# Splitting w_out beside the last token block, with the GLU parts in two buffers and chunk 1 loaded behind them

## What is computed

```python
h = rmsnorm(x, norm_pre_mix);  proj = h @ w_in
u, z, xbc, dt_raw, qk, v, i_raw, f_raw, o_raw = split(proj)
y_a = s5_mixer(u, ...)      # 32 groups x 16 channels, complex state; then g * sigmoid(g @ w_glu + b_glu)
y_b = ssd_mixer(z, xbc, dt_raw, ...)                 # 12 heads x 64, 2 groups, state 128, chunks of 128
y_c = mlstm_mixer(qk, v, i_raw, f_raw, o_raw, ...)   # 6 heads, keys 64, values 128
x = x + rmsnorm(concat[y_a, y_b, y_c] @ w_out, norm_post_mix)
h = rmsnorm(x, norm_pre_ffn)
out = x + rmsnorm((silu(h @ w_gate) * (h @ w_up)) @ w_down, norm_post_ffn)
```

## Time and profile before

| | |
|---|---|
| Timed runs | 3061.14, 3063.23, 3067.11 us |
| Profiled execution | 3071.86 us, span on the core 3070.1 us |
| Busy share of the span | TensorE 94%, VectorE 62%, ScalarE 39%, GpSimd 13% |
| VectorE in tenths, slices of 77 us | 3 from 998 to 1074 us, 4 from 1074 to 1151 us |
| Weight split L1576, mean of its group | 1345 ns |
| Load of `m_bc`, median to landing | 6.9 us |
| Token stage, last tile | about 1123.5 us |
| Mixers | 1124 to about 1490 us |

### The profile page before, as it was taken

The page is one execution under the profiler, slowest core; times in us unless marked ns, Lnnn a source line. Parts: engine busy times, 40 slices in busy tenths (PEclk is TensorE's granted clock), DMA queues, the critical chain, the costliest instruction groups (busy, mean ns, idle before and its releaser), DMA issues. The chain is left out here.

```text
span 3070.1 us, 36078 instructions
## 1 busy us (share of the span) xinstructions
PE 2893.7 (94%) x13608; PEld 2329.9 (76%) x13608; DVE 1918.2 (62%) x2608; ACT 1200.5 (39%) x2000; POOL 390.4 (13%) x495
## 2 busy tenths in 40 slices
PE   7999999799999888999699859999999999999998
PEld 4788887577777666777488748888878888888887
DVE  4677877575652348888334467666676666556756
ACT  5322222354343344544234343333443333444543
POOL 0000000013440225665012100000000000000100
PEclk9999999899999988999799979999999999999999
DMA  4222433336666737776568654444543222776863
GB/s 149 66 66 87 128 128 104 117 133 204 215 202 187 237 103 248 265 278 245 203 250 307 235 195 168 158 158 158 182 174 130 103 103 105 270 247 195 297 192 110
DMA packets 295289, 545.14 MB, mean 178 GB/s; under 512 B 59308, under 2 KB 150860, under 8 KB 286284
## 3 DMA queue, kind: packets, MB, share of 16 engines
q1 hardware_dynamic: 263356, 437.69, 42.5%
q0 software_dynamic: 24704, 75.52, 6.8%
q10 hardware_dynamic: 7056, 29.63, 2.4%
HBM read 358.30 MB, written 184.44 MB: 177 GB/s over the span
## 5 line engine op out<-in xcount | busy, mean ns | idle before, releaser
L2530 PE MATMUL f_banks<-f_bop,f_w_op 128*128 128x512 f32 x3696 | 841.2, 390 | 31.5 <-DVE f_w_op L2357 29.5
L2530 PEld LDWEIGHTS f_banks<-f_bop,f_w_op 128*128 128x128 f32 x3696 | 695.4, 188 | 177.3 <-DVE f_w_op L2357 29.9
L2538 PE MATMUL f_banks<-f_d_op 128*128 128x512 f32 x1848 | 419.0, 389 | 0.0
L2538 PEld LDWEIGHTS f_banks<-f_d_op 128*128 128x128 f32 x1848 | 346.8, 188 | 72.0
L2421 DVE TENSOR_TENSOR f_d_op<-f_d_raw,f_d_op 128x1024 fp32r<-128x1024 f32 x154 | 187.5, 1225 | 149.0 <-ACT f_d_op L2274 148.3
L1708 PE MATMUL t_banks<-t_w_hi,h_hi 128*128 128x512 f32 (+1 forms) x640 | 249.4, 390 | 26.4 <-DVE t_w_lo L1576 26.4
L640 PE MATMUL c_banks<-h_hi,c_w_hi 128*128 128x512 f32 x640 | 255.7, 400 | 0.0
L640 PE MATMUL c_banks<-h_hi,c_w_lo 128*128 128x512 f32 x640 | 249.9, 391 | 0.0
L640 PE MATMUL c_banks<-h_lo,c_w_hi 128*128 128x512 f32 x640 | 249.1, 389 | 0.0
L2274 ACT ACTIVATE f_d_op<-f_d_raw 128x1024 fp32r<-128x1024 f32 x154 | 162.9, 1061 | 198.3 <-PE f_banks L2538 161.6
L1708 PE MATMUL t_banks<-t_w_lo,h_hi 128*128 128x512 f32 (+1 forms) x640 | 239.6, 374 | 0.0
(11 more groups left out here) (350 smaller groups left out, 4620.6 us busy)
## 6 DMA issues: line engine op xcount, KB each, us to landing
f_raw<-in_w_gu SPq DMA_DIRECT2D x88, 512.0 KB, 6.4
sop<-f_a SPq DMA_DIRECT2D x154, 256.0 KB, 2.0
f_d_raw<-sop SPq DMA_DIRECT2D x154, 256.0 KB, 2.8
t_raw<-in_w_tok SPq DMA_DIRECT2D x72, 512.0 KB, 4.4
f_d_raw<-top SPq DMA_DIRECT2D x88, 256.0 KB, 3.8
m_bc<-rows SPq DMA_DIRECT2D x16, 1152.0 KB, 6.9
f_d_raw<-in_w_dn SPq DMA_DIRECT2D x66, 256.0 KB, 3.0
o_y_hi<-y_hi SPq DMA_DIRECT2D x16, 1024.0 KB, 5.1
```

What stands on the lines that cost most here:

```text
L2530: last = nc.tensor.matmul(bank[:, g, :], w_op[:, t % W_RING, w, cols], bop[:, s, h, k, :], start=begins and k == 0 and j == 0, stop=k == 3 ...
L2538: last = nc.tensor.matmul(banks[:, bank, :], d_op[:, d % D_RING, s, tok], d_op[:, d % D_RING, w, :], start=k == 0 and j == 0, stop=k == FU ...
```

## The change

**GLU parts.** `y_hi` and `y_lo` have two buffers each, by the parity of the part; `y` is written into the buffer of `y_lo` and overwritten by the difference. The semaphore of the stores is split by parity, and a part waits for the store of part n - 2 instead of n - 1.

**w_out.** The six pieces are loaded, copied and split in the token stage: load g at slot 116 + 4g on SyncE, copy and split at slot 118 + 4g on ScalarE and VectorE, behind whatever else the slot holds. There is one raw buffer instead of two, so a load waits for the split before it; the other half of `gate_rows` becomes `m_va` of even chunks.

**Chunk 1.** `m_w_hi` and `m_w_lo` must now lie clear of the token stage. In their place the second buffers of `bc`, `ch`, `tk`, `zo`, `va`, and xde, xskip, h and others, overlap with it. So chunk 1 is loaded in `rest()`, and GpSimd's xde and xskip of chunk 0 and VectorE's memset of h follow the last tile.

**Waits.** `tokens_done` is now the tiles' products alone. A new `stores_done` (tiles copied and stored, GLU parts stored) is awaited by SyncE before the loads of chunk 1, by ScalarE before the first squares, by GpSimd behind the first products, and by VectorE before the first write of `y`.

```diff
@@ mixer_memory @@
-        sb("pad_a", [P, 110])
...
+        sb("pad_a", [P, 640])
+        bc1, ch1 = sb("bc1", [P, NBC, P]), sb("ch1", [P, CT - CH0, P])
...
+        w_hi, w_lo = sb("w_hi", [P, NT, NB], F32R), sb("w_lo", [P, NT, NB], F32R)
...
+        tk1, zo1, va1 = sb("tk1", [P, CTT * P]), sb("zo1", [P, XW + VW]), sb("va1", [P, HM, DA])
@@ mixers @@
+    w_raw = gate_rows[:, 0:WM * NB].rearrange("p (k m) -> p k m", k=WM)
+    va = gate_rows[:, WM * NB:WM * NB + HM * DA].rearrange("p (h v) -> p h v", h=HM), va1
+    AHEAD, AHEAD_MASK, AHEAD_EXP, AHEAD_W = 112, 124, 132, 116
...
+    def split(slot, part):
+        g, r = divmod(slot - AHEAD_W - 2, 4)
+        if r == 0 and 0 <= g < NT // WM:
+            part(g)
@@ sync @@
         def load_w(g):
-            if g >= 2:
-                sp.wait_ge(wlo_ok, g - 1)
-            sp.dma_start(w_raw[:, g % 2], ...).then_inc(w_in[g % 2], 16)
+            if g:
+                sp.wait_ge(wlo_ok, g)
+            sp.dma_start(w_raw, ...).then_inc(w_in, 16)
         def ahead(slot):
...
-            elif slot == AHEAD + 8:
-                load_bc(1)
-                load_ch(1)
...
+            g, r = divmod(slot - AHEAD_W, 4)
+            if r == 0 and 0 <= g < NT // WM:
+                load_w(g)
         def rest():
+            tokens_done(sp)
+            stores_done(sp)
             for c in range(1, TT):
...
+                load_bc(c)
+                load_ch(c)
+                if c == 1:
+                    sp.wait_ge(set_ok, 2)
+                load_va(c)
+                load_tk(c)
+                load_zo(c)
@@ scalar @@
         def ahead(slot):
+            if slot == AHEAD + 5:
+                act.wait_ge(const_in, 16 * 7)
+            split(slot, upper_w)
         def rest():
             for c in range(TT + 2):
-                if c < 3:
-                    upper_w(2 * c)
-                    upper_w(2 * c + 1)
...
+                if c == 0:
+                    stores_done(act)
@@ gpsimd @@
-            elif slot == AHEAD_EXP:
-                products(0)
         def rest():
             tokens_done(pool)
             for c in range(TT):
-                if c:
-                    products(c)
+                products(c)
+                if c == 0:
+                    stores_done(pool)
+                    nc.gpsimd.memset(va[1][:, :, DV:DA], 1.0).then_inc(set_ok, 1)
@@ vector @@
         def ahead(slot):
...
+            split(slot, lower_w)
         def rest():
             tokens_done(dve)
+            nc.vector.memset(h_state[:], 0.0).then_inc(h_ok, 1)
...
+                if c == 0:
+                    stores_done(dve)
                 step(dve, tt(yg, bank_y[:, :, 0:GW], off[:] ..., add), diag_read, c + 1)
...
-                if c < 3:
-                    lower_w(2 * c)
-                    lower_w(2 * c + 1)
@@ phase_tokens @@
         def tokens_done(eng):
             eng.wait_ge(tile_mm, TILES_T * BLK)
+
+        def stores_done(eng):
             eng.wait_ge(evac_ok, TILES_T * BLK)
             tiles_sent(eng, BLK)
-            eng.wait_ge(part_sent, 32 * UT * BLK)
+            for b in range(2):
+                eng.wait_ge(part_sent[b], 32 * UT * BLK // 2)
@@ glu_gate (ScalarE) @@
-                if n:
-                    act.wait_ge(part_sent, 32 * n)
-                nc.scalar.activation(y_hi.bitcast(F32R), y, ACT.Copy).then_inc(yhi_ok, 1)
+                if n >= 2:
+                    act.wait_ge(part_sent[n % 2], 32 * (n // 2))
+                nc.scalar.activation(y_hi[n % 2].bitcast(F32R), y_lo[n % 2], ACT.Copy).then_inc(yhi_ok, 1)
@@ glu (VectorE) @@
-                if n:
-                    dve.wait_ge(yhi_ok, n)
-                    dve.wait_ge(ylo_ok, n)
+                if n >= 2:
+                    dve.wait_ge(part_sent[n % 2], 32 * (n // 2))
+                y = y_lo[n % 2]
...
-                if n:
-                    dve.wait_ge(part_sent, 32 * n)
-                tt(y_lo.bitcast(F32R), y, y_hi, sub).then_inc(ylo_ok, 1)
+                tt(y.bitcast(F32R), y, y_hi[n % 2], sub).then_inc(ylo_ok, 1)
```

More of the change, by code:

```diff
@@ L733, in mixer_memory @@
[L733 to L739, removed]
+        c_state = sb("c", [P, HP, DA])
@@ new lines, in mixer_memory @@
+        sb("pad_a", [P, 640])
+        bc1, ch1 = sb("bc1", [P, NBC, P]), sb("ch1", [P, CT - CH0, P])
+        c_old, den, stat = sb("c_old", [P, HP, DA]), sb("den", [P, 3, 2, HP]), sb("stat", [P, 4, NG])
+        sb("pad_b", [P, 88])
+        w_hi, w_lo = sb("w_hi", [P, NT, NB], F32R), sb("w_lo", [P, NT, NB], F32R)
+        y_hi, y_lo = sb("y_hi", [P, 2, NT, P], F32R), sb("y_lo", [P, 2, NT, P], F32R)
+        xde, xskip, off, h_state, h_old = (sb(s, [P, HS, HD]) for s in ("xde", "xskip", "off", "h", "h_old"))
@@ L968, in masked @@
             for h in MASKED:
-                part = bc[:, c % 2, h:h + MH]
+                part = bc[c % 2][:, h:h + MH]
                 nc.gpsimd.tensor_tensor(part, part, mask[:].unsqueeze(1).to_broadcast([P, MH, P]), ALU.add
@@ L1036, in ahead @@
                 blocks_done(dve)
-                chain(nc.vector.memset(h_state[:], 0.0))
-                chain(nc.vector.memset(c_state[:], 0.0))
-                dve.sem_inc(h_ok, 1)
-                dve.sem_inc(c_ok, 1)
+                nc.vector.memset(c_state[:], 0.0).then_inc(c_ok, 1)
+            elif slot == AHEAD + 5:
+                dve.wait_ge(const_in, 16 * 7)
+            split(slot, lower_w)
         def rest():
             tokens_done(dve)
-            dve.wait_ge(const_in, 16 * 7)
-            dve.wait_ge(set_ok, 1)
+            nc.vector.memset(h_state[:], 0.0).then_inc(h_ok, 1)
+            dve.wait_ge(h_ok, 1)
+            dve.wait_ge(c_ok, 1)
             for c in range(TT + 1):
@@ L1160, in rest @@
                         rows = slice(e * DK, (e + 1) * DK)
-                        last = mm(bank_x[:, e, i * P:(i + 1) * P], ch[rows, b, K_T + i, :], ch[rows, b, Q_T + i, :],
+                        last = mm(bank_x[:, e, i * P:(i + 1) * P], ch[b][rows, K_T + i, :], ch[b][rows, Q_T + i, :],
                                   start=True, stop=True)
@@ L1166, in rest @@
                 for g in range(NG):
-                    last = mm(bank_y[:, 0, g * P:(g + 1) * P], ch[:, b, B_T[g], :], ch[:, b, C_T[g], :], start=True, stop=True)
+                    last = mm(bank_y[:, 0, g * P:(g + 1) * P], ch[b][:, B_T[g], :], ch[b][:, C_T[g], :], start=True, stop=True)
                 last.then_inc(cb_mm, 1)
@@ L1172, in rest @@
                 for g in range(NG):
[L1173 removed]
+                    last = mm(bank_x[:, g, 0:GW], ch[b][:, C_T[g], :],
                               h_state[:].rearrange("p h d -> p (h d)")[:, g * GW:(g + 1) * GW], start=True, stop=True)
@@ L1196, in rest @@
                         rows = slice(e * DK, (e + 1) * DK)
-                        last = mm(bank_y[:, e, i * DA:(i + 1) * DA], ch[rows, b, Q_T + i, :], c_state[rows, i, :],
+                        last = mm(bank_y[:, e, i * DA:(i + 1) * DA], ch[b][rows, Q_T + i, :], c_state[rows, i, :],
                                   start=True, stop=True)
@@ L1204, in rest @@
                     e, i = h % 2, h // 2
-                    last = mm(bank_x[:, e, i * DA:(i + 1) * DA], bc[:, b, HS + h, :], va[:, b, h, :], start=True, stop=True)
+                    last = mm(bank_x[:, e, i * DA:(i + 1) * DA], bc[b][:, HS + h, :], va[b][:, h, :], start=True, stop=True)
                 last.then_inc(pv_mm, 1)
@@ L1276, in phase_tokens @@
         g = at(2048, UT * NB).rearrange("p (k t) -> p k t", k=UT)
-        gate, y = at(4096, NB), at(4608, NB)
-        y_hi, y_lo = (at(5120 + i * NB, NB) for i in range(2))
+        gate = at(4096, NB)
+        y_lo, y_hi = ([at(4608 + (2 * i + j) * NB, NB) for i in range(2)] for j in range(2))
         glu_bank = side[:, 0:2]
@@ L1413, in send_y @@
                 sp.wait_ge(ylo_ok, n + 1)
-                for dst, part in ((yhi_dram, y_hi), (ylo_dram, y_lo)):
-                    sp.dma_start(dst[QT * b:QT * (b + 1), :, m, :].rearrange("n p t -> p n t"), chunks(part)).then_inc(part_sent, 16)
+                for dst, part in ((yhi_dram, y_hi[n % 2]), (ylo_dram, y_lo[n % 2])):
+                    sp.dma_start(dst[QT * b:QT * (b + 1), :, m, :].rearrange("n p t -> p n t"), chunks(part)).then_inc(part_sent[n % 2], 16)
             load(0, 0)
```

91 lines of the change are left out of this document (35 added, 56 removed).

## The result

The changed kernel takes 3041.23 us (median of 4 runs, 3038.15 to 3047.99) against 3065.17 us of the kernel before on the same chip (3061.14 to 3068.74): ratio 0.9925, 95% interval 0.9907 to 0.9944, so 23.9 us faster. The forecast was 3029.7, range 3021 to 3045. The profiled execution has a span of 3046.2 us, 23.9 less than before.

What follows compares the result with a forecast made beforehand. TensorE, busy 94% of the span, could gain only from its waits and lower clock; VectorE paced the mixers. 18.3 + 15.7 - 0.5 = 33.5 us off the 3063.2 us median gave 3029.7 us, range 3021 to 3045.

Steps and rivals of the forecast that it cites:

- Rival D: Token stage: late w_out loads hold ScalarE, each of six units waits on t_w_lo; slower, 3072 us; chance 4%.
- C: Same places: TensorE waits as long for another reason, the loads; below 6 us of change, 3060 us; chance 5%.
- B: Transfers replace the waits: g late in both blocks, chunk 1 lands after 20 us; 23.5 us gained, 3040; chance 30%.
- A: As forecast, every removed wait having a named holder: 3030 us, own range 3024 to 3036; chance 57%.
- the base: Whole kernel: the profiled execution's waits assumed in the timed median too, 3063.2 us, though the profile stood 8.6 us above it.
- Part 1: Token stage, GLU parts in two buffers: TensorE's waits and the low clock behind them go, 18.3 us gained.
- the residue: Token stage: what stays of block 2's wait for g with its clock, 2.5 us of 20.8.
- Part 2: End of token stage: copying and splitting w_out beside the last token block costs TensorE 0 us.
- Part 3: Mixers' first chunks: 60.0 us instead of 74.1 for three, with the earlier first operation 15.7 us gained.
- The start: Mixer chunk 0: VectorE's first L1057 waits for its product instead of stores, 1.6 us gained.
- Part 4: Chunk 0: GpSimd's products xde and xskip meet VectorE after the last token tile, 0.5 us lost, bounds 0 and 3.

Runs made afterwards that it cites:

- e2: The changed kernel with the two buffers of the GLU parts undone, back to one buffer; 3058.20 us, ratio 0.9977.
- g1: The changed kernel with only chunk 0's m_tk and m_zo loaded at slot 122 instead of 116; 3036.78 us, ratio 0.9909.
- e4: The changed kernel with w_out's loads and splits four slots later and chunk 0's m_tk and m_zo loaded at slot 122 instead of 116; 3036.12 us, ratio 0.9903.
- e3: The changed kernel with all six loads and splits of w_out four slots later; 3040.62 us, ratio 0.9919.
- f3: The changed kernel with GpSimd's two products of a chunk held back until VectorE has finished y of the chunk before; 3025.51 us, ratio 0.9865.
- f4: e4 with GpSimd's products also held back until VectorE has finished y of the chunk before; 3018.76 us, ratio 0.9846.
- g3: f4 with a chunk's first product waiting for m_ch alone, the other loads awaited where they are used; 3017.19 us, ratio 0.9848.
- e1: The kernel before with only the two buffers of the GLU parts added; 3049.55 us, ratio 0.995.
- g2: The changed kernel with the stores again awaited together with the last token tile, before the mixers; 17.0 us less than the kernel before, a single timed run.

## Why the prediction was right in its range, and 11.5 us off

**The mechanism was right.** The waits on `t_w_lo`, the wait on `m_w_lo` and ScalarE's waits for stores went, block 3's `g` came in time and the splits of w_out left the mixers at almost no cost to TensorE. Rival D is out: TensorE has no wait on `t_w_lo`; one load of w_out held ScalarE for 8.1 us, another for 1.7. C is out. The time is that of B (3040), but B's mechanism holds in block 2 only: block 3's `g` was 0.36 us late, and chunk 1 was complete after 15.7 us, not 20. It lies outside A's own range (3024 to 3036). That it falls in the wide range, and on B's number, is in part luck, since the largest error below stands in no rival.

**The step that failed most: the base.** "I assume the same waits there." I saw that the profiled execution stood 8.6 us above the median and carried its waits over to the median. The second trace of before is 6.5 us shorter in exactly this stretch, 4.1 in the chunks and 2.3 in the token end. 33.5 us was thus a gain against an unusual execution. (Against the timed gain of 23.9 us it is 9.6 too much; the other 1.9 of the 11.5 us are the fourth timed run of the kernel before, which moved its median from 3063.23 to 3065.17.)

**Part 1: the residue was mis-sized.** I kept 2.5 us for block 2's `g`; it is 3.11 us of wait and 3.07 of slow products, 6.2. I looked at the new load of w_out, and it was the old loads of `m_tk` and `m_zo`, which the earlier `g` now stands right behind, with the new load between. For block 3 I let `g` go out 8 us earlier, where the row of the wait supports 6.2; it went out at 1059.80 instead of 1069.48, and the wait was 0.36 us. In traces part 1 gives 17.2 us alone (143.0 to 125.8), and 14.0 to 14.8 inside the change (e2 against after), for 18.3 forecast.

**Part 2: zero for TensorE, nearly.** ScalarE stood 8 us, and no wait on `t_w_lo` came of it. In g1, with all loads of w_out in place and `m_tk` and `m_zo` moved, the token end is as short as in e4 (124.7 and 124.6). With these two ahead, the first load of w_out costs 1.4 to 2.2 us by way of `g` (e3's 129.1 us against 130.5 and 131.3), which the timed medians do not resolve (3040.62 and 3041.23).

**Part 3: 15.7 us forecast.** The start gave 1.3 of 1.6. The chunks take 62.0 and 62.8 us in the two traces, for 60.0; chunks 1 and 2 are the late ones. In chunk 1 I took 1 us for GpSimd beside VectorE's small operations, with 18.2 us else; the row of after, VectorE and then GpSimd:

```profile
1146.53 0.66 DVE L1098 TENSOR_SCALAR m_stat<-m_stat 128x2 f32<-128x2 f32 x1
...
1147.67 0.94 DVE L1103 SCALAR_TENSOR_TENSOR m_den<-m_num 128x6 f32<-128x6 f32 x1
1148.65 1.40 DVE L1104 TENSOR_TENSOR m_den<-m_den,m_tok_cols 128x6 f32<-128x6 f32 x1
```

```profile
1148.55 1.48 POOL L981 TENSOR_TENSOR m_xskip<-m_tk,m_skip 128x768 f32<-128x768 f32 x1
```

L1098, L1103 and L1104 take 3.0 us here, and 0.79 in the same chunk of before (0.45, 0.17 and 0.17), where the splits of w_out kept VectorE busy until most of the products had passed: 2.2 us, not 1. (The 0.56 and 0.17 us that the expectation of f3 gives for chunk 1 are misread.) In f3, without the products beside them, chunk 1 takes 18.6 us. In chunk 2 L1098 takes 1.00 us and VectorE waits 2.69 us for TensorE's L1180. TensorE's granted clock was 0.81, 0.68 and 0.83 in three of the 10 us stretches from 1120 to 1160; what that adds is not shown. Against the second trace of before part 3 is worth 9.3 us (72.5 to 63.2 in e2), and timed 7.2. Chunk 0 was right at 20.06 (20.65 in the second trace) for the wrong reason: I had the first product of chunk 1 wait for `m_zo`, and f4 and g3 show that this wait, 4.1 and 0.4 us, moves the chunk by 0.2 us. `m_zo` matters by another way, the next part.

**Part 4: 0.5 us for a meeting on L1064.** It was not slowed (0.95 us), but it did not meet them either: it starts at 1114.71, and the second product ends at 1114.56. So this run does not decide whether L1064 can be held; in f3, where it meets the last 0.3 us of a product in the later chunks, it takes 1.10 us. What met GpSimd in chunk 0 was L1109, 2.2 us, beside the products of chunk 1, as I had not considered: these come late because the loads do.

The forecast less these: 33.5 - 6.5 (base) - 3.7 (residue) - 0.4 (block 3) - 2.0 (chunks) - 0.3 (start) = 20.6 us; the first trace of after shows 21.8 in this stretch, the second 20.2. The timed gains, 23.9 and 21.7 us, are 3.3 and 1.1 more, which nothing here accounts for. Behind chunk 3 the unchanged rest takes 1866 to 1872 us in the ten traces that leave it alone, and the first trace of after is the longest of them. One of its places is a stretch at a granted clock of 0.91 in a late stage, where the second trace of after has 1.00 (length, TensorE busy, clock, DMA share, GB/s):

```profile
2213.00:2233.00 20.00, 17.83 (x70) 0.91 0.52 172
```

**Left open.** How much of a wait costs the clock behind it. In blocks 2 and 3, waits of 1.87 us (e1) and 3.14 us (second trace of before) were followed by a GLU group of 3.67 us, close to full speed; waits of 2.66 (e3, g2), 3.34 (before), 4.44 (second trace of before) and 4.55 us (e2) by one of 5.37; and waits of 3.11 to 3.79 us (both traces of after, f3, e2 and before) by 6.45 to 6.66. That a wait can cost up to twice its length is shown, when it does is not, and its length alone does not tell. Nor is it shown why issuing `g` is slow behind `m_tk` and `m_zo`; the order was moved, not the mechanism.

## What to carry to other kernels

Before a gain is subtracted from a median, see how far the profiled execution stands above it: the excess may lie in the very waits that are to be removed, and a second trace of the kernel before settles it. When a transfer is made earlier, list what already stands ahead of it in the queue at its new time, the old transfers too. And where VectorE paces a loop, look for its tiny operations that end together with one of GpSimd's: one added wait on GpSimd gave 17.6 us here, and the whole change 21.7 beside it.

## What was not expected of the hardware

A VectorE operation of 0.17 us takes 1.13 us when a product of GpSimd (1.47 us) is under way, while L1057 and L1063 (0.55 and 0.95 us each, one input in PSUM) lose nothing beside the same products in f3. The issue of three loads of `g` (256 KB each) for block 2 takes 3.4 us or 7.0 us, by what was issued before and how long before; for block 3, with no large load of chunk 0 near, it took 4.3 us in after and 5.1 in before, so these loads are not all of it. Two executions of one kernel differed by 6.5 us in a stretch of 220 us.
